# A second set of split-operand buffers in a hybrid decoder step (gated linear attention, RG-LRU, mixture of experts)

## What is computed

```
proj = x @ w_in                      # q, k, v, output gate g, low-rank gate, xr, merge gates m
o    = GLA(q, k, v, decay)           # 4 heads, chunks of 64 tokens, matrix state; 8 decode states
o    = LayerNorm_per_head(o) * silu(g)
h    = RG_LRU(conv4(xr))             # h_t = a_t h_{t-1} + b_t, elementwise recurrence
merged = sigmoid(m0) * (o @ w_branch[0]) + sigmoid(m1) * (h @ w_branch[1])
x    = LayerNorm(alpha * x + merged @ w_o)
y    = LayerNorm(alpha * x + MoE(x)) # 32 experts, top 4, clamped SwiGLU
```

## Time and profile before

| | |
|---|---|
| median of 3 runs | 1287.6 us (1284.17 to 1291.08) |
| the profiled execution | 1284.81 us, its span 1282.8 us |
| TensorE busy | 1157.2 us (90%) |
| VectorE busy | 390.0 us (30%) |
| ScalarE busy | 292.1 us (23%) |
| DMA, mean over the span | 356 GB/s |
| chain that ended last | PE 42%, DMA 24%, SyncE's queue 23%, VectorE 4%, ScalarE 2% |

### The profile page before, as it was taken

How to read it: one execution, slowest core, us unless ns; L and a number is a source line. 1 busy time by engine, 2 the same in 40 slices (tenths; PEclk the granted TensorE clock), 3 DMA queues, 4 the chain that set the end, 5 groups by cost and what they waited for, 6 DMA issues and landing times.

```text
span 1282.8 us, 18268 instructions
## 1 busy us (share of the span) xinstructions
PE 1157.2 (90%) x7064; PEld 617.4 (48%) x7064; DVE 390.0 (30%) x719; ACT 292.1 (23%) x522; POOL 19.3 (2%) x41
## 2 busy tenths in 40 slices
PE   8999999989899999988888898989898989888895
PEld 7998878985444343333333343333333333333341
DVE  4888477755202202020202121120202020202025
ACT  5685444335210110101010101111010101010101
POOL 1000020000000000000000000000000000000000
PEclk9999999999899999999999999999999999999998
DMA  9745476866599999999999999999999999999992
GB/s 280 222 131 175 156 245 226 306 233 264 225 418 418 417 418 418 417 418 418 418 417 417 417 417 417 418 418 419 417 418 418 417 418 418 419 417 417 415 416 89
DMA packets 118343, 456.83 MB, mean 356 GB/s; under 512 B 10408, under 2 KB 49336, under 8 KB 85312
## 3 DMA queue, kind: packets, MB, share of 16 engines
q1 hardware_dynamic: 115440, 446.03, 87.7%
q0 software_dynamic: 2864, 10.26, 2.5%
HBM read 450.30 MB, written 5.95 MB: 356 GB/s over the span
## 4 chain that ended last, share of the span: by engine, by line
PE 42%; DMA 24%; SPq 23%; DVE 4%; issue 4%; ACT 2%; DVEq 0%; ACTq 0%
DMA gu_w<-in_moe_w_gu 23%; PE pool L566 15%; SPq L390 14%; PE pool L855 10%; SPq L385 7%; PE pool L890 6%; PE ub L815 5%; ACT arena L1130 1%; PE ob L869 1%; DMA dn_w<-in_w_in 1%; PE pool L883 1%; ACT wh L924 1%; PE ub L869 1%; DVE wl L1169 1%; PE ub L792 0%
## 5 line engine op out<-in xcount | busy, mean ns | idle before, releaser
L855 PE MATMUL pool<-gu_w,arena 128*64 128x512 f32 x2048 | 467.4, 599 | 42.5 <-DMA gu_w<-in_moe_w_gu 41.5
L855 PEld LDWEIGHTS pool<-gu_w,arena 128*64 128x64 f32 x2048 | 139.4, 137 | 351.7 <-issue 211.1
L1589 DVE TENSOR_SCALAR arena<-pool 128x512 f32<-128x512 f32 x32 | 22.1, 692 | 750.1 <-PE pool L855 749.0
L890 PE MATMUL pool<-dn_w,arena 128*64 128x512 f32 x1024 | 226.8, 595 | 21.6 <-ACT arena L1130 21.6
L566 PE MATMUL pool<-xh,wh 128*128 128x264 f32 x568 | 165.8, 292 | 7.0 <-DVE xl_most L1162 5.5
L566 PE MATMUL pool<-xh,wl 128*128 128x264 f32 x568 | 162.5, 286 | 0.0
L890 PEld LDWEIGHTS pool<-dn_w,arena 128*64 128x64 f32 x1024 | 70.7, 137 | 157.1 <-issue 127.9
L566 PE MATMUL pool<-xl_most,wh 128*128 128x264 f32 x497 | 142.8, 287 | 0.0
L1126 ACT ACTIVATE arena<-arena 128x512 f32<-128x512 f32 x32 | 20.2, 630 | 496.6 <-DVE arena L1589 496.6
L566 PEld LDWEIGHTS pool<-xh,wh 128*128 128x128 f32 x568 | 109.0, 192 | 13.6 <-issue 11.2
L566 PEld LDWEIGHTS pool<-xh,wl 128*128 128x128 f32 x568 | 108.4, 191 | 0.0
(11 more groups left out here) (308 smaller groups left out, 720.3 us busy)
## 6 DMA issues: line engine op xcount, KB each, us to landing
gu_w<-in_moe_w_gu SPq DMA_DIRECT2D x256, 1024.0 KB, 20.4
dn_w<-in_moe_w_down SPq DMA_DIRECT2D x256, 512.0 KB, 21.5
dn_w<-in_w_in SPq DMA_DIRECT2D x24, 1024.0 KB, 5.5
dn_w<-in_w_branch SPq DMA_DIRECT2D x8, 1024.0 KB, 5.5
gu_w<-in_state_gla POOLq DMA_DIRECT2D x8, 512.0 KB, 6.0
out_gla_sample<-gu_w POOLq DMA_DIRECT2D x8, 512.0 KB, 4.9
dn_w<-in_w_o SPq DMA_DIRECT2D x4, 1024.0 KB, 5.8
arena<-in_xT SPq DMA_DIRECT2D x2, 528.0 KB, 5.4
```

The costliest lines, as they stand in the source:

```text
L855: last = mm(out, xg[:, k, j * CAP:(j + 1) * CAP], gu_w[:, k, cols], start=False, stop=(k == NB - 1))
L890: last = mm(DOWN[s * CAP:(s + 1) * CAP, :], act_t[:, k % 4, k // 4 * CAP:(k // 4 + 1) * CAP], dn_w[:, k, s * HF:(s + 1) * HF], start=(k == ...
```

## The change

A second pair of buffers `xh2`, `xl2` is laid over slots 4 and 7 of the arena. Stages 0 and 2 keep the old pair, stages 1 and 3 use the new one. `xl2` lies where `hs` lies: each block of `hs` is replaced by its low part. With that:

- ScalarE makes the high part of block n-2 of `hs` behind the merge gate of m_n (n = 2 to 7), and the last two before m8; it waits for `rg_done` there.
- VectorE makes the low parts of `hs`, two at a time, behind the four weight parts that follow the last update of the recurrence's matrix state (the last of the four steps of its loop).
- In the b0 loop both engines split `merged` of block n-1 behind the weight part of project n, and block 7 at the end.
- TensorE's projects read the pair that belongs to their stage. Their number and order are the same, 24 matmuls each.

```diff
@@ buffers
+        arena_at = gu_at + 4 * (NB * 2 * F + NB * D + NB * T + T)
+
+        xh2, xl2 = (nc.alloc_sbuf_tensor_at(f"x{part}2", [P, NB, T], F32R, offset=arena_at + 4 * i * SLOT)
+                    for part, i in (("h", 4), ("l", 7)))
+        operands = [([xh[:, k, :] for k in range(NB)], xl),
+                    ([xh2[:, k, :] for k in range(NB)], [xl2[:, k, :] for k in range(NB)])]
@@ TensorE, project
                     if name in ("b10", "b00", "wo0"):
                         pe.wait_ge(x_lo, stage * NB + k + 1)
-                    for w, x in ((h, xh[:, k, :]), (h, xl[k]), (l, xh[:, k, :])):
-                        last = mm(bank(name)[:, 0:T], w[:, k, :], x, start=(k == 0 and w is h and x is not xl[k]),
-                                  stop=(k == NB - 1 and w is l))
+                    high, low = (part[k] for part in operands[stage % 2])
+                    mm(bank(name)[:, 0:T], h[:, k, :], high, start=(k == 0), stop=False)
+                    mm(bank(name)[:, 0:T], h[:, k, :], low, start=False, stop=False)
+                    last = mm(bank(name)[:, 0:T], l[:, k, :], high, start=False, stop=(k == NB - 1))
@@ ScalarE
-            def high_operand(k, src):
-                nc.scalar.copy(xh[:, k, :], src[:, k, :]).then_inc(x_hi, 1)
+            def high_operand(k, src, stage):
+                nc.scalar.copy(operands[stage % 2][0][k], src[:, k, :]).then_inc(x_hi, 1)
...
                 merge_gate(n)
-            sc.wait_ge(rg_done, 2)
+                if n >= 2:
+                    sc.wait_ge(rg_done, 2)
+                    high_operand(n - 2, hs, 1)
+            for k in range(NB - 2, NB):
+                high_operand(k, hs, 1)
             sc.wait_ge(braw_in, 48)
...
-            wait_filled(sc, f"m{2 * NB - 1}")
-            for k in range(NB):
-                high_operand(k, hs)
             sc.wait_ge(od_full, DEC)
...
             for n in range(NB):
                 after(f"b0{n}")
-            for n in range(NB):
-                wait_drained(sc, f"b0{n}")
-                high_operand(n, merged)
+                if n:
+                    wait_drained(sc, f"b0{n - 1}")
+                    high_operand(n - 1, merged, 3)
+            wait_drained(sc, f"b0{NB - 1}")
+            high_operand(NB - 1, merged, 3)
@@ VectorE
                 v.wait_ge(x_hi, stage * NB + k + 1)
-                tt(xl[k], src[:, k, :], xh[:, k, :], ALU.subtract).then_inc(x_lo, 1)
+                high, low = operands[stage % 2]
+                tt(low[k], src[:, k, :], high[k], ALU.subtract).then_inc(x_lo, 1)
...
                     for m in ((0,), (1, 2), (3,), (4, 5, 6, 7))[2 * t + pair]:
                         late_part(M0 + SPLITS + m)
+                        if t and pair:
+                            for k in range(2 * m - 8, 2 * m - 6):
+                                low_operand(k, hs, 1)
...
                 late_part(M0 + SPLITS + NB + b)
-            for k in range(NB):
-                low_operand(k, hs, 1)
             v.wait_ge(o_read, 2)
             norm_stats([0, 1])
...
                 late_part(split_of[f"b0{n}"] + SPLITS)
-            for k in range(NB):
-                low_operand(k, merged, 3)
+                if n:
+                    low_operand(n - 1, merged, 3)
+            low_operand(NB - 1, merged, 3)
```

More of the change, by code:

```diff
@@ L554, in project @@
                         pe.wait_ge(x_lo, k + 1)
-                        for x in (xh[:, k, :], xl[k]):
-                            mm(bank(name)[:, 0:T], h[:, k, :], x, start=(k == 0 and x is not xl[k]), stop=False)
+                        for i in range(2):
+                            mm(bank(name)[:, 0:T], h[:, k, :], operands[0][i][k], start=(k == 0 and i == 0), stop=False)
                     pe.wait_ge(w_lo, 1)
@@ L942, in _ @@
                 for k in range(4 * half, 4 * half + 4):
-                    high_operand(k, x_raw)
+                    high_operand(k, x_raw, 0)
                 high_part(half)
@@ L1067, in _ @@
                 wait_drained(sc, f"ot{n}")
-                high_operand(n, oT)
+                high_operand(n, oT, 2)
             for n in range(NB):
                 after(f"b0{n}")
-            for n in range(NB):
-                wait_drained(sc, f"b0{n}")
-                high_operand(n, merged)
+                if n:
[3 more added lines that the diff above has]
+            high_operand(NB - 1, merged, 3)
             for n in range(NB - 3):
```

## The result

| | before | changed |
|---|---|---|
| median of 15 runs each | 1286.79 us (1281.62 to 1291.08) | 1280.13 us (1277.51 to 1285.2) |
| ratio | | 0.9948, interval 0.9934 to 0.9963 |
| profiled execution, span | 1282.8 us | 1276.0 us |

The gain is 6.7 us, by the interval 4.8 to 8.5. Forecast were -6.2 us and 1281.4 us, with a range of 1276.5 to 1287.5 us.

The account below looks back on a forecast made before the run. The experts' weights' stream, started by TensorE's progress, was taken to bound the kernel. Stage 1 (-2.75), the early split's cost (+0.2) and stage 3 (-3.64) summed to -6.2 us, so 1281.4 us, range 1276.5 to 1287.5 us.

Parts of the forecast that it names:

- What bounds the kernel: Experts' weights' stream sets the last 800 us and starts from TensorE's progress; a microsecond saved before wo7 reaches the end.
- Rival 5: Weights' stream begins when it did, or low parts are still late: gain hidden, 1287.6 us; chance 0.06.
- Stage 1: hs split early, b10 to b13: gain 2.75 us and not 4.2, since b13 waits for VectorE's weight part.
- The new pause: TensorE's wait ahead of b13 for VectorE's weight part, forecast at about 1.7 us.
- The clock ahead of b13: No clock fall in the pause ahead of b13, argued from one of 1.87 us; otherwise 1.44 us lost.
- rival 2: Pause ahead of b13 lowers the clock: b13 takes 4.36 us, gain 4.8 us, 1282.8 us; chance 0.15.
- What the early split costs: Later first decode product, partly given back in later turns: between nothing and 0.7 us, taken as 0.2.
- six of the eight fit there: Six of hs's eight subtractions fit VectorE's idle time ahead of weight parts; the last two delay decode arithmetic.
- Stage 3: merged split block by block, at wo0: gain 3.64 us from the shorter wait and the vanished low stretch.
- Sum: Whole kernel: -2.75 + 0.2 - 3.64 = -6.2 us, with bounds of -4.25 and -7.6.
- Rival 4: The low clock stretch at 228 us goes too: 1280.0 us; chance 0.08.
- Rival 6: Slower: added 0.6 us lowers the clock in the decode turns and it stays down, 1296 us; chance 0.04.

Follow-up runs that it names:

- e5: Changed kernel plus 24 unread 128x128 matmuls on TensorE between b07 and wo0; 1284.04 us, 0.998 of the kernel before.
- e4: Changed kernel with hs's low parts where high parts are ready, statistics in decode turns 5 to 7, square root earlier; 1276.87 and 1277.42 us.
- e3: Changed kernel with hs's low parts moved into decode turns 4 to 7, two in each; 1279.97 us, 0.9951 of the kernel before.
- a2: The changed kernel again, unaltered, one profiled execution; span 1283.3 us.
- e6: e4 plus idle matmuls in two TensorE pauses, ahead of the first chunk's products and the first expert's token gathering; 1275.82 us, again 1274.7 us.

## Why the prediction was right, point by point

**What bounds the kernel.** Right: the weights' stream hangs on TensorE, and what the mixer saves arrives whole (last column of the table, e5). Rival 5 falls.

**Stage 1.** Right to 0.02 us: 2.75 forecast, 2.77 measured, for the reason given. Only VectorE's eight subtractions leave the list to b13; e4, which empties that list, gets 1.74 us more. The new pause measures 1.50, not 1.7, since b10 to b12 end at 211.14 - 1.50 = 209.64, 9.00 us after their start at 200.64. The forecast's 3 x 2.92 = 8.76 counts from start to start and leaves out that the last matmul lasts 0.28 us; b13's start is not touched by it.

**The clock ahead of b13.** It did not fall in any of the six profiles with this pause (b1 is 25.62 or 25.63 in the table's five and in e5's). But the reason was weak. I argued from one pause of 1.87 us that had not brought the clock down; the same pause did so in the next profile. So no fall was partly luck: a pause of this length is a chance and not a limit, and rival 2 deserved its 0.15.

**What the early split costs.** This term was mis-sized: 0.2 us forecast with bounds of 0 and 0.7, 0.91 measured, outside the bounds. The step that failed is "six of the eight fit there". I counted VectorE's idle time ahead of the weight parts and did not look when the high parts come: block 5's is made behind m7, one project later than the low part that needs it. VectorE's wait of 1.64 us stood ahead of m7's weight part, and the first decode product came 1.35 us late, counted from m5, where 0.6 was forecast. By VectorE's list about 0.7 of it is the missing operand (m7's weight part starts at 163.32, its `wh` was done at 162.62) and the rest the last two subtractions, which had been foreseen. The later turns gave 0.44 back, about as much as was forecast (0.4). e3 takes all eight subtractions away from there and the term is gone (47.00); no run takes away the operand's wait alone.

**Stage 3.** Right: 3.64 forecast, 3.59 measured, with a pause of 0.58 us at block 6 where 0.6 was expected, and no low clock at wo0. The prediction's clock of 0.76 around each pause was shown for the first alone; the profile of the kernel before has it around the second too:

```profile
257.00:264.00 7.00, 4.17 (x24) 3.99 (x23) 4.84 (x11) 3.56 (x9) 1.08 (x2) 0.76 0.86 290
```

**Sum.** By the steps -5.45 us instead of -6.2: the early split cost 0.7 us more than forecast. The medians say -6.7, and the steps' sum lies within their interval (-4.8 to -8.5). So that the median came out beyond the forecast, and not short of it, is luck and no support for the term of 0.2. Fewer low stretches in other places explain little of the surplus of 1.2 us. The mean clock is 0.9885 over the changed kernel's 15 runs and 0.9856 over 53 runs of the kernel before, which were measured beside the experiments: 0.0029 more. The two low stretches at b10 and wo0 that the steps already count make 2 x 7 x (1 - 0.76) / 1283 = 0.0026 of it (an estimate from the stretches of 7 us at 0.76). The rest is worth some 0.4 us. Rival 4 (the stretch at b00 gone) was true of two of the changed kernel's three profiles and false of the third.

**Rival 6.** The fall in the decode turns did occur once, in a2, at a cost of 3.1 us. It did not keep itself up: the granted clock was 0.50 from 168.5 to 175 us and 1.00 in the turns from 176 us on. As a price of the new wait of 1.5 us it is a chance, not a constant.

## What to carry to other kernels

When a step is moved earlier, check for every instruction of it not only that its engine is idle there, but that its operand exists there: one instruction waiting for an operand holds all behind it on its engine. When a wait is removed, follow each engine that joins at the next meeting point; the gain is the smallest of their gains (2.77 of 4.2 us here), and the rest is got only by shortening the list that is late next (e4). Where the times of single runs scatter by more than the change is worth, compare step by step between landmarks of one engine: here that resolves 0.1 us where fifteen runs resolve 2.

## What the runs showed of the hardware that was not expected

**The clock.** It falls at the same pause in one execution and not in the next (0.83 and 1.00 over the ten us from 125), after pauses of 1.4 to 1.9 us. The falls that the steps resolve cost 1.2 us (b00, 43.16 against 42.00) to 3.1 us (a2's decode turns), and the three profiles of one program spread over 7.9 us. Among the changed kernel's fifteen runs the one with the lowest mean clock, 0.983, is the slowest, 1285.2 us, and those at 0.991 and 0.992 are among the fastest, 1277.5 to 1278.1.

**A lower clock that costs little.** e6's second profile was granted 0.95 outside its low stretches, 0.94 in the mean. Its span was 1276.6 us against 1271.7 in e6's first. At 0.95 TensorE is busy 785 us instead of 764 between 345 and 1190 us, and DMA moves the same 418 GB/s. e6's first profile:

```profile
345.00:1190.00 845.00, 764.46 (x4310) 309.55 (x4308) 137.91 (x243) 109.93 (x234) 0.00 (x0) 1.00 1.02 418
```

Its second:

```profile
345.00:1190.00 845.00, 784.96 (x4312) 317.44 (x4310) 138.08 (x243) 109.96 (x234) 0.00 (x0) 0.95 1.02 418
```

TensorE's waits for the experts' weights fall from 41.6 to 21.4 us (from 340 us on) and take up the difference. The experts' part waits for the weights and not for TensorE.
